# Two whole transposes and copies in halves in place of eight transposes, and idle matmuls, in a delta-rule solve

## The reference

```
def _gated_delta_chunked(q, k, v, g, beta):       # both directions, 4 heads
    ...
    lower = jnp.where(strict, jnp.einsum('bhnid,bhnjd->bhnij', kb, k) * decay, 0.0)
    tmat = lower + jnp.eye(c, dtype=jnp.float32)   # c = 64
    rhs = jnp.concatenate([v * beta[..., None], kb * jnp.exp(g)[..., None]], axis=-1)
    sol = lax.linalg.triangular_solve(tmat, rhs, left_side=True, lower=True, unit_diagonal=True)
    ...
    def step(state, inp):                          # over the chunks
        v_new = u_i - jnp.einsum('bhck,bhkv->bhcv', w_i, state)
        o_i = jnp.einsum('bhck,bhkv->bhcv', qg_i, state) + jnp.einsum('bhij,bhjv->bhiv', qk_i, v_new)
        state = state * gl_i[..., None, None] + jnp.einsum('bhck,bhcv->bhkv', kg_i, v_new)
        return state, o_i
```

## Time and profile before

| what | value |
|---|---|
| median of 3 runs | 1807.08 us (1807.48, 1807.08, 1802.1) |
| profiled execution: time, span | 1801.51 us, 1799.7 us |
| PE busy | 1641.1 us, 91% of the span |
| VectorE, ScalarE, POOL busy | 858.7, 716.5, 590.7 us |
| chain that ended last, by engine | PE 77%, VectorE 13%, ACT 6%, issue 3% |

### The profile page before, as it was taken

One profiled execution on the slowest core, in us unless ns is written; L12 is line 12 of the kernel. 1 busy time (PEld: TensorE's weight loads), 2 busy tenths in 40 slices (PEclk: granted clock), 3 DMA queues, 4 the chain that ended last, 5 costly groups with the idle time before them and its releaser, 6 DMA issues.

```text
span 1799.7 us, 28936 instructions
## 1 busy us (share of the span) xinstructions
PE 1641.1 (91%) x11842; PEld 1331.1 (74%) x11842; DVE 858.7 (48%) x1570; ACT 716.5 (40%) x1115; POOL 590.7 (33%) x312
## 2 busy tenths in 40 slices
PE   6999999988989989989999987099899899999997
PEld 3788888866878767768877756097688688888886
DVE  3101365476340356476757657964434454444113
ACT  5325213254352624354644968014433522222222
POOL 1122323193313221453024301062234244444442
PEclk9999999999999999999999999599999999999999
DMA  9444311310122111402522210001121132233332
GB/s 343 165 142 148 119 40 49 118 37 13 59 101 68 65 60 60 141 1 90 169 98 94 73 45 2 1 2 59 59 71 48 61 104 94 94 103 97 103 108 71
DMA packets 43851, 151.66 MB, mean 84 GB/s; under 512 B 4560, under 2 KB 7888, under 8 KB 43600
## 3 DMA queue, kind: packets, MB, share of 16 engines
q1 hardware_dynamic: 40176, 140.76, 23.5%
q10 hardware_dynamic: 3552, 9.13, 1.4%
HBM read 145.67 MB, written 4.19 MB: 83 GB/s over the span
## 4 chain that ended last, share of the span: by engine, by line
PE 77%; DVE 13%; ACT 6%; issue 3%; DMA 1%; POOL 0%; SPq 0%; DVEq 0%; ACTq 0%
PE wide_ps L1983 53%; PE wide_ps L2040 4%; DVE xn L1434 1%; PE wide_ps L2058 1%; PE wide_ps L2281 1%; PE pair_ps L2099 1%; PE duo_ps L2080 1%; DVE xn L1687 1%; PE duo_ps L2742 1%; DMA ring<-weights 1%; ACT xn L909 1%; PE wide_ps L2723 1%; PE wide_ps L2005 1%; DVE proj L1352 1%; PE wide_ps L2165 1%
## 5 line engine op out<-in xcount | busy, mean ns | idle before, releaser
L590 POOL TENSOR_TENSOR ring_r<-ring,scratch_r 128x1024 fp32r<-128x1024 f32 x168 | 411.5, 2450 | 935.6 <-ACT scratch_r L770 862.4
L1983 PE MATMUL wide_ps<-xn_r,scratch_r 128*128 128x512 f32 x1272 | 468.4, 368 | 0.0
L1983 PE MATMUL wide_ps<-work_r,scratch_r 128*128 128x512 f32 (+1 forms) x1109 | 425.2, 383 | 6.6 <-POOL ring_r L590 4.7
L1983 PE MATMUL wide_ps<-work_r,ring_r 128*128 128x512 f32 (+1 forms) x1109 | 408.8, 369 | 0.0
L770 ACT ACTIVATE scratch_r<-ring 128x1024 fp32r<-128x1024 f32 x190 | 200.9, 1058 | 511.7 <-PE wide_ps L1983 443.7
L1983 PEld LDWEIGHTS wide_ps<-xn_r,scratch_r 128*128 128x128 f32 x1272 | 240.3, 189 | 43.9 <-issue 5.4
L1983 PEld LDWEIGHTS wide_ps<-work_r,scratch_r 128*128 128x128 f32 x1109 | 209.3, 189 | 53.3 <-issue 10.6
L1983 PEld LDWEIGHTS wide_ps<-work_r,ring_r 128*128 128x128 f32 x1109 | 208.8, 188 | 36.4
L1983 PE MATMUL wide_ps<-proj_r,scratch_r 128*128 128x512 f32 x634 | 211.9, 379 | 0.0
L1983 PEld LDWEIGHTS wide_ps<-proj_r,scratch_r 128*128 128x128 f32 x634 | 119.0, 188 | 22.7 <-ACT xn L754 0.4
L754 ACT ACTIVATE proj<-wide_ps 128x512 f32<-128x512 f32 (+2 forms) x86 | 56.7, 659 | 193.4 <-PE wide_ps L1983 187.6
(11 more groups left out here) (481 smaller groups left out, 2887.3 us busy)
## 6 DMA issues: line engine op xcount, KB each, us to landing
ring<-weights SPq DMA_DIRECT2D x254, 512.0 KB, 3.7
h<-tokens SPq DMA_DIRECT2D x4, 768.0 KB, 10.1
h<-tokens ACTq DMA_DIRECT2D x1, 3072.0 KB, 10.4
out<-h ACTq DMA_DIRECT2D x1, 2048.0 KB, 7.3
h<-out ACTq DMA_DIRECT2D x1, 2048.0 KB, 9.6
out<-h SPq DMA_DIRECT2D x16, 128.0 KB, 1.8
proj<-weights SPq DMA_DIRECT2D x2, 512.0 KB, 14.7
h<-mem ACTq DMA_DIRECT2D x1, 1024.0 KB, 13.1
```

The lines of the kernel that those rows point to most:

```text
L590: pool.tensor_tensor(as_r(wt), wt, as_r(w_lead(m)).bitcast(F32), ALU.subtract).then_inc(w_split, 1)
L1983: last = pe.matmul(bank[:, a:b], wt[:, cols], as_r(x[:, a:b]), start=n == 0 and p == 0, stop=n == len(k_order) - 1 and p == 2)
```

## The change

The eight large transposes become two on all 128 partitions. The first writes the transposed squares to a scratch, `tri_back`, in columns of the constants' tile that lie behind `tri_tmp`; the second writes the plain ones to `tri_pack`. From there the squares are copied to their places, in two halves (`part`: 16 of the 32 squares, for p = 0, 1 and p = 2, 3) of four copies each, one for each group of 32 partitions: by ScalarE into `tri_across`, by VectorE into `tri_straight`. Each copy is on 32 partitions by 512 columns. Half-products 0 and 1 now wait for the first half of both engines' copies, half-products 2 and 3 for the second; `half_masked(0)` and POOL's masks wait for all of VectorE's, as `TRI_READY[1]` is now the count of both transposes and eight copies. PE gets six f32 matmuls of 128x128 by 128x448 with a zero as the stationary operand, ahead of half-products 0, that write to a PSUM bank nobody reads before half-products 0 overwrite it. They wait until the solver has done step j = 24 of 30 (`SQ - 8`).

```diff
+RUN_COLS = 448
-        tri_tmp = const[:, CONST_COLS["rot_pair"][0]:CONST_COLS["rot_pair"][0] + 256]
+        tri_at = CONST_COLS["rot_pair"][0]
+        tri_tmp = const[:, tri_at:tri_at + 256]
+        tri_back = const[:, tri_at + 256:tri_at + 1280].rearrange("p (m c) -> p m c", c=SQ)
+        square_from = lambda v, part, g: v[SQUARE[g], 16 * part:16 * part + 16, :]
+        square_place = lambda v, part, g: v[SQUARE[g]].rearrange("p (m t) -> p m t", t=HD)[:, 16 * part:16 * part + 16, SQ * (g % 2):SQ * (g % 2) + SQ]
+        solve_near_end = []
...
-        TRI_READY = [TRI_TURNED + len(SQUARE) * (n + 1) for n in range(2)]
+        TRI_READY = [TRI_TURNED + 2 + len(SQUARE) * (n + 1) for n in range(2)]
+        TRI_SET = [TRI_COPIED + 2 + len(SQUARE) * (n + 1) for n in range(2)]
...
             for v in (tri_across, tri_straight):
                 act.activation(v, zero[:, 0:1].broadcast_to([P, 2048]), ACT.Copy).then_inc(tri_placed, 1)
+            act.wait_ge(tri_turned, TRI_TURNED + 1)
+            act.wait_ge(tri_placed, TRI_COPIED + 2)
+            for part in range(2):
+                for g in range(len(SQUARE)):
+                    act.activation(square_place(tri_across, part, g), square_from(tri_back, part, g), ACT.Copy).then_inc(tri_placed, 1)
...
-                for n, (to, frm) in enumerate(((tri_across, tri_solve.rearrange("p c r -> p r c")), (tri_straight, tri_solve))):
-                    dve.wait_ge(tri_placed, TRI_COPIED + n + 1)
-                    for g, run in enumerate(SQUARE):
-                        at = SQ * (g % 2)
-                        dve.transpose(to[run].rearrange("p (m t) -> p t m", t=HD)[:, at:at + SQ, :], frm[run]).then_inc(tri_turned, 1)
+                    if j == SQ - 8:
+                        solve_near_end.append(dve_count[0])
+                dve.transpose(tri_back.rearrange("p m t -> p t m"), tri_solve.rearrange("p c r -> p r c")).then_inc(tri_turned, 1)
+                dve.transpose(tri_pack.rearrange("p m t -> p t m"), tri_solve).then_inc(tri_turned, 1)
+                dve.wait_ge(tri_turned, TRI_TURNED + 2)
+                dve.wait_ge(tri_placed, TRI_COPIED + 2)
+                for part in range(2):
+                    for g in range(len(SQUARE)):
+                        dve.tensor_copy(square_place(tri_straight, part, g), square_from(tri_pack, part, g)).then_inc(tri_turned, 1)
...
+            def keep_running(ps, count):
+
+                for _ in range(count):
+                    pe.matmul(ps[:, 0:RUN_COLS], zero[:, :], const[:, 0:RUN_COLS], start=True, stop=True)
...
             def half_products(p):
 
-                if p == 0:
-                    pe.wait_ge(dn_g_used, 2 * NLAT)
-                pe.wait_ge(tri_turned, TRI_READY[min(p, 1)])
+                pe.wait_ge(tri_turned, TRI_READY[p // 2])
+                pe.wait_ge(tri_placed, TRI_SET[p // 2])
...
+            pe.wait_ge(dn_g_used, 2 * NLAT)
+            pe.wait_ge(dve_chain, solve_near_end[0])
+            keep_running(dn_bank(0), 6)
             for p in range(5):
```

## The result

| | before | after |
|---|---|---|
| runs | 1807.48, 1807.08, 1802.1, 1808.94, 1804.97 us | 1799.34, 1795.11, 1796.57, 1793.6, 1799.0 us |
| median | 1807.08 us | 1796.57 us |
| ratio | | 0.9943, 95% interval 0.9926 to 0.9960 |
| span of the profiled execution | 1799.7 us | 1797.6 us |

The change makes the kernel 0.57% faster, 10.3 us of 1807. The forecast was 1792.5 us, the range 1788.6 to 1800.5. A second measurement of the same kernel gave 0.9923 (0.9910 to 0.9936), 13.9 us.

What follows compares the result with a forecast made beforehand. Bound: VectorE's eight transposes, then PE in the last inverse level. Transposes and copies -8.26 us and level -3.76 make -12.0, from 1804.5 to 1792.5 us; range 1788.6 to 1800.5.

Steps and rivals of the forecast that it cites:

- Transposes: VectorE ahead of the last level: two 128x1024 transposes take 3.97 us in place of 15.96, saving 11.99 us.
- VectorE's copies: Eight 32x512 SBUF copies behind the transposes take 3.69 us without overlap, 2.8 with overlap, 5.8 at the upper price.
- the cast's 427 over the PSUM copy's 691: Price in ns of one VectorE copy: 427 taken; 691 was the slow-copies rival, 2.1 us more, chance 0.08.
- the hold between groups: A VectorE copy on another 32-partition group waits until earlier ones finish, so eight copies take 3.69 us, not 2.8.
- ScalarE's copies: Eight copies at 0.65 us each from 1153.4, done at 1158.6, hidden behind VectorE's with 0.4 us to spare.
- Idle products: Six f32 products on PE from 1147.75 raise the clock between 1151 and 1153, end near 1154.5 and cost nothing.
- rival (a): PE's clock is low again when the last level begins; the level takes 13.90 us, gain 8.4 us; chance 0.32.
- Stage: Transposes to end of last level: 8.26 us saved up to the copies' end, 3.76 in the level, 12.0 together.
- POOL: POOL's masks wait for the last copy and end at 1168.9; its slack shrinks from 5.00 to 1.4 us and holds.
- the upper price of the idle products: On PE, six at 1.79 us make 10.7 us, ending at 1158.4; half-products then end at 1160.3, costing 0.4 us.
- all work moves with it: Behind the last level no queue of SP or POOL changes its order, so the 12.0 us gain stays whole.
- The base: Time of before that the 12.0 us was taken from: 1804.5 us, the mean of four runs including the profiled one.

Runs made afterwards that it cites:

- experiment 10: The kernel after with both halves of each 32-partition group copied one behind the other on VectorE, all half-products waiting for all its copies; eight copies 3.12 us, stage 20.0 us.
- experiments 1 and 6: The former: after without the six idle products, stage 19.0 us. The latter: before with all half-products waiting for all eight transposes, stage 29.3 us.
- experiment 11: After with four more idle products, two behind each transpose, and VectorE's first mask ahead of its second half of copies; stage 17.3 us, ratio 0.9930.
- the filled gap: After with four more idle products on PE, two behind each of the two transposes; stage 17.9 us, ratio 0.9944.

## Why the prediction was right

The time lies in the range and the mechanism is the one forecast, by its own steps:

- *Transposes.* 3.83 us against 3.97 and 0.04 for the wait. A transpose does cost by its columns; writing at a stride of 32 words is as dear as at 64.
- *VectorE's copies.* 3.56 us against 3.69; 418 ns each and 0.45 us apart. The choice of the cast's 427 over the PSUM copy's 691 was right, and so was the hold between groups (experiment 10). The Trainium skill's rule in "VectorE: DVE Perf Modes", section "Two Vector instructions with no wait between them", gave the nearer of the two sums.
- *ScalarE's copies.* 5.19 us, 627 ns each; done 0.2 us ahead of VectorE's (1167.17 against 1167.33), not 0.4.
- *Idle products.* Half right. They cost nothing, the clock rose 3.2 us behind their start (3.0 to 3.8 in all ten traces that have them) and they took 6.3 us in place of about 6.7. The forecast that the clock then holds came true in one of two traces. In the other it fell as half-products 1 began: close to rival (a), but not at its price.
- *Price of rival (a).* This is the term that was mis-sized. I let the level run its 13.90 us of before if the clock was low, 3.6 us above the forecast. It costs 0.8 us when the clock falls behind half-products 0 (18.7 against 17.9), and 1.1 when there are no idle products at all (19.0). In before only one phase of half-products stood ahead of the inverse products; in after there are two, and with two together the clock came up 4.0 to 4.3 us behind their start in place of 7.6 to 8.0 (experiments 1 and 6). What the 11.4 and 12.1 us of the stage owe to each part: 11.0 to 11.1 come without any idle product, 0.3 or 1.1 with the six.
- *Stage.* 12.0 us forecast; 11.4 and 12.1 measured. Of these, 8.6 come up to the end of the last copy (7.4 us behind the solver, in both traces, where half-products 1 of before started 16.0 us behind it); 8.3 were forecast. The level behind it took 11.2 us where the clock fell and 10.4 where it held, against 14.1 of before: 2.9 or 3.7 us, with 3.8 forecast.
- *POOL.* The slack shrank to 2.0 us in the trace in which the clock fell, and to 1.2 in the second, in which it held as the forecast of 1.4 supposes. It was not used up in either; experiment 11 shows how little more it takes. In the second trace:

```profile
1175.70 0.31 POOL L678 MEMSET xn<- 64x256 f32 x1 [1.24 <-PE duo_ps L2659]
```

- *A slip that nothing rests on.* For the upper price of the idle products the clock never rises. The two phases of half-products would then take 1.66 us each and end at 1161.7, not at the 1160.3 of the prediction, which has them at 0.93. No run shows this case.
- *Behind the stage.* Here the prediction was wrong in a small thing: "all work moves with it". The rest took 619.0 and 619.3 us in the traces of after, 618.3 in both of before, so 0.7 to 1.0 us are given back. In after the clock falls once more some 70 us behind the solver, in a stretch where PE has little to do:

```profile
1227.00:1231.00 4.00, 1.91 (x8) 1.05 (x6) 3.90 (x5) 1.58 (x2) 2.33 (x1) 1.00 0.00 0
1231.00:1234.50 3.50, 2.65 (x6) 1.90 (x7) 3.26 (x5) 0.00 (x0) 0.25 (x1) 0.54 0.00 0
```

In before the same work, 2.9 us later, kept its clock:

```profile
1229.90:1233.90 4.00, 1.86 (x7) 1.05 (x6) 3.90 (x5) 1.54 (x2) 2.39 (x1) 1.00 0.00 0
1233.90:1237.40 3.50, 1.79 (x7) 1.18 (x8) 3.21 (x5) 0.00 (x0) 0.19 (x1) 1.00 0.00 0
```

  Of the 14 traces the eight with this fall have 618.8 to 620.4 us behind the last update, the six without it 618.1 to 618.4. That is a correlation over all traces, not a test: no run moved the fall alone.
- *The base.* 1804.5 us, the mean of four runs with the profiled one, was low: before had medians of 1807.08, 1806.36, 1807.07 and 1805.53 in four measurements. With the first of these the forecast is 1795.1 us, 1.5 from the median measured.

What stays open: how often the clock holds over the gap with six idle products, and what decides it. Two traces are too few for a share, and the ratios of after, of the version without idle products and of the filled gap overlap.

## What to carry to other kernels

When an operation costs by its columns, that is by the elements on each partition, splitting it over groups of partitions multiplies its price: do it once on all partitions into a scratch, and let two engines place the parts with cheap copies, the half that is needed first ahead. Measure a change of 10 us in a kernel of 1800 by the stage between two fixed events in the trace, since the code ahead of it moved by 8.6 us between executions. A warm-up that ends before the work begins may be lost; before paying for one, look at how soon the work's own first phases bring the clock up.

## What the runs showed of the hardware

- A copy of VectorE between SBUF tiles and an operation of POOL that reads SBUF took turns: eight copies took 10.27 us beside POOL's masks, 3.56 without; seven of them 1.38 us each, one to each mask. Two transposes of VectorE and three masks of POOL side by side hardly disturbed each other (2.03 and 1.97 us, 2.01 and 1.91 alone; 1.25 us a mask, 1.24 alone).
- Independent copies of VectorE started 0.11 us later, about, where the group of 32 partitions changes.
- The granted clock of PE rose 4.0 and 4.3 us behind the start of two phases of half-products, but 7.6 to 8.0 us behind the start of one phase followed by inverse products, though PE was busy without a gap all that time.
- The same kernel kept the clock at 1.00 over 2.49 us of idle PE in one execution and lost it behind 2.83 us in another; behind 4.0 to 5.4 us it was low in all five traces.
